# The last level of a block inverse in 32 by 32 blocks, inside the scan of a recurrent model

## The reference, cut to what matters

```
D_MODEL = 1024; SEQ = 512; DEPTH = 2; CHUNK = 64; HEAD_SIZE = 64; N_HEADS = 8

def wkv7_scan(r, w, k, v, kk, a):
    # state (B, H, N_v, N_k):
    # S_t = S_{t-1} (diag(w_t) - kk_t^T (a_t*kk_t)) + v_t k_t^T ;  y_t = S_t r_t
    def step(state, inp):
        r_t, w_t, k_t, v_t, kk_t, a_t = inp
        sk = einsum('bhvk,bhk->bhv', state, kk_t)
        state = (state * w_t[:, :, None, :] - sk[..., None] * (a_t * kk_t)[:, :, None, :]
                 + v_t[..., None] * k_t[:, :, None, :])
        return state, einsum('bhvk,bhk->bhv', state, r_t)
    ...
```

## Time and profile before

| | us |
|---|---|
| median of three runs | 3784.06 |
| lowest, highest | 3781.48, 3784.39 |
| the profiled execution, its own time | 3784.52 |
| its span, first to last instruction | 3782.7 |

### The profile page before, as it was taken

The page is one execution under the profiler, slowest core; times in us unless marked ns, Lnnn a source line. Parts: engine busy times, 40 slices in busy tenths (PEclk is TensorE's granted clock), DMA queues, the critical chain, the costliest instruction groups (busy, mean ns, idle before and its releaser), DMA issues. The chain is left out here.

```text
span 3782.7 us, 57931 instructions
## 1 busy us (share of the span) xinstructions
PE 3664.8 (97%) x24033; PEld 3028.9 (80%) x24033; DVE 2174.3 (57%) x2934; ACT 1367.3 (36%) x1537; POOL 0.2 (0%) x4
## 2 busy tenths in 40 slices
PE   7999999999999999999999998999999998899998
PEld 6788888888877888888887768888887768888887
DVE  6898466774369964667634565553234575553233
ACT  5554433432264544343323341133223351123223
POOL 0000000000000000000000000000000000000000
PEclk9999999999999999999999999999999999999999
DMA  3322223553322222245522420123232320032321
GB/s 112 87 73 62 78 89 110 202 189 122 94 78 81 67 68 78 94 151 189 198 89 71 132 79 26 36 101 99 90 100 81 111 99 26 25 111 89 100 94 73
DMA packets 272985, 364.68 MB, mean 96 GB/s; under 512 B 22428, under 2 KB 218640, under 8 KB 271504
## 3 DMA queue, kind: packets, MB, share of 16 engines
q1 hardware_dynamic: 247824, 311.45, 25.7%
q10 hardware_dynamic: 24960, 50.33, 3.8%
HBM read 351.79 MB, written 9.96 MB: 96 GB/s over the span
## 5 line engine op out<-in xcount | busy, mean ns | idle before, releaser
L248 PE MATMUL banks<-act_hi,w_hi 128*128 128x512 f32 x4208 | 1675.2, 398 | 32.1 <-issue 9.9
L250 PE MATMUL banks<-act_hi,w_lo 128*128 128x512 f32 x4208 | 1647.9, 392 | 0.0
L249 PE MATMUL banks<-act_lo,w_hi 128*128 128x512 f32 x4208 | 1647.5, 392 | 0.0
L170 DVE TENSOR_TENSOR w_lo<-w_raw,w_hi 128x2048 fp32r<-128x2048 f32 (+1 forms) x280 | 629.4, 2248 | 666.8 <-ACT w_hi L164 662.6
L248 PEld LDWEIGHTS banks<-act_hi,w_hi 128*128 128x128 f32 x4208 | 795.5, 189 | 237.1 <-issue 59.0
L250 PEld LDWEIGHTS banks<-act_hi,w_lo 128*128 128x128 f32 x4208 | 794.7, 189 | 169.9
L249 PEld LDWEIGHTS banks<-act_lo,w_hi 128*128 128x128 f32 x4208 | 796.0, 189 | 165.1 <-issue 4.3
L164 ACT ACTIVATE w_hi<-w_raw 128x2048 fp32r<-128x2048 f32 (+1 forms) x280 | 526.5, 1881 | 932.8 <-PE banks L250 891.4
L2064 DVE SCALAR_TENSOR_TENSOR arena<-arena,small 128x512 f32<-128x512 f32 (+1 forms) x168 | 126.3, 752 | 15.6 <-issue 4.3
L248 PE MATMUL banks<-w_hi,act_hi 128*128 128x256 f32 x384 | 110.3, 287 | 3.2 <-DVE w_lo L170 3.2
L249 PE MATMUL banks<-w_lo,act_hi 128*128 128x256 f32 x384 | 108.6, 283 | 0.0
(11 more groups left out here) (363 smaller groups left out, 3592.7 us busy)
## 6 DMA issues: line engine op xcount, KB each, us to landing
w_raw<-in_w_in SPq DMA_DIRECT2D x98, 1024.0 KB, 5.4
w_raw<-in_ffn_up SPq DMA_DIRECT2D x48, 1024.0 KB, 5.4
arena<-in_ada_w ACTq DMA_DIRECT2D x24, 2048.0 KB, 8.0
w_raw<-in_w_gu SPq DMA_DIRECT2D x44, 1024.0 KB, 5.0
w_raw<-in_ffn_down SPq DMA_DIRECT2D x24, 1024.0 KB, 4.8
w_raw<-in_w_down SPq DMA_DIRECT2D x20, 1024.0 KB, 5.0
w_raw<-in_w_out SPq DMA_DIRECT2D x16, 1024.0 KB, 4.9
w_raw<-in_w_branch SPq DMA_DIRECT2D x12, 1024.0 KB, 5.0
```

What stands on the lines that cost most here:

```text
L170: self.core.nc.vector.tensor_tensor(view(self.lo[:, s]), view(self.raw[:, s]), view(self.hi[:, s]).bitcast(FP32), ALU.subtract)\
L248: nc.tensor.matmul(out, wh, ah, start=first, stop=False)
L249: nc.tensor.matmul(out, wh, al, start=False, stop=False)
L250: return nc.tensor.matmul(out, wl, ah, start=False, stop=last)
```

## The change

At the last level (size 32) only one quarter of a head's matrix changes, and only the transpose of X is read later. The new code treats that level by itself, behind a loop over the first four:

- W is computed as one 32 x 32 product per head instead of one of 64 x 64. `quarters(h)` gives the upper and the lower 32 partitions of a head; the product reads the upper and writes the lower.
- VectorE copies that quarter into W for each of the two `h` (two instructions on 32 partitions with 4 blocks of 32 columns each) instead of one masked instruction on 128 x 256, and signals through a drain instead of with the instruction.
- The product into the first half of X is gone. The one into the transpose is 32 x 32 per head.
- VectorE subtracts it from the upper right quarter of the transpose, again in two instructions of 32 partitions.

The count and the order of the semaphores stay as they were.

```diff
+        def quarters(h):
+            return slice(64 * h, 64 * h + 32), slice(64 * h + 32, 64 * h + 64)
+
@@ pe_part
-                for n, lv in enumerate(LEVELS):
+                for n, lv in enumerate(LEVELS[:4]):
...
+                for cc in (0, 1):
+                    pe.wait_ge(x_ok, 12 * g + 8 + cc + 1)
+                    for pr, h in pairs:
+                        top, low = quarters(h)
+                        col, o = (cc * NP + pr) * CH, pr * CH
+                        last = nc.tensor.matmul(ps[low, w_bank[cc], o:o + 32], AT[top, col + 32:col + 64],
+                                                XX[cc][top, o:o + 32], start=True, stop=True)
+                    last.then_inc(w_ps, 1)
+                for cc in (0, 1):
+                    pe.wait_ge(w_ok, 10 * g + 8 + cc + 1)
+                    for pr, h in pairs:
+                        top, low = quarters(h)
+                        col, o = (cc * NP + pr) * CH, 256 + pr * CH + 32
+                        last = nc.tensor.matmul(ps[top, x_bank[cc], o:o + 32], W[low, col:col + 32],
+                                                XX[cc][low, o:o + 32], start=True, stop=True)
+                    last.then_inc(x_ps, 1)
@@ dve_part
-                for n, lv in enumerate(LEVELS):
+                for n, lv in enumerate(LEVELS[:4]):
...
+                left = lambda v: as3(v)[:, :, 0:32]
+                right = lambda v: as3(v)[:, :, 32:64]
+                for cc in (0, 1):
+                    dve.wait_ge(w_ps, 10 * g + 8 + cc + 1)
+                    for h in (0, 1):
+                        low = quarters(h)[1]
+                        nc.vector.tensor_copy(left(half(W, cc)[low]), left(ps[low, w_bank[cc], 0:256]))
+                    dve.drain().then_inc(w_ok, 1)
+                for cc in (0, 1):
+                    dve.wait_ge(x_ps, 10 * g + 8 + cc + 1)
+                    for h in (0, 1):
+                        top = quarters(h)[0]
+                        xt = right(XX[cc][top, 256:512])
+                        tt_(xt, xt, right(ps[top, x_bank[cc], 256:512]), ALU.subtract)
+                    dve.drain().then_inc(x_ok, 1)
```

## The result

| | before | after |
|---|---|---|
| median, us | 3784.28 (20 runs, 3779.97 to 3788.84) | 3790.41 (20 runs, 3786.82 to 3793.81) |
| profiled execution, us | 3784.52 | 3789.69 |

The ratio is 1.0017 with a 95% interval of 1.0011 to 1.0023. The change makes the kernel 6.1 us slower, where 5.2 us faster was forecast. The forecast was wrong in its sign, and the time lies outside its range (3775.5 to 3786).

The account below looks back on a forecast made before the run. TensorE and VectorE alternate in the last level, so savings there should reach the end in full: 3.53 - 2.88 = 0.65 us, 8 times, 5.2 us; 3784.5 - 5.2 = 3779.3 us (50%), own range 3776.5 to 3782, 8 in 10 3775.5 to 3786.

Parts of the forecast that it names:

- The sum: Timeline of the new last level: 2.88 us in place of 3.53, 0.65 us saved 8 times, 5.2 us.
- VectorE's pair: Two last-level instructions on different 32-partition groups, taken at 0.58 us with no overlap and no pause; ends 0.50 and 0.70.
- The row's overlap of 0.08 us: Profile row of two VectorE instructions on the same partitions, starting 0.34 us apart though one takes 0.42.
- (b): Rival, 16%: VectorE's pairs in the last level overlap as on equal partitions, 6.6 to 7.8 us faster.
- (c): Rival, 14%: VectorE's second instruction waits as behind a drain, or small tiles cost more; 1.4 us faster to 2.3 slower.
- The burst: TensorE's 16 records per chunk in the last level, taken at 0.73 us; range 0.52 to 0.73, or 1.16.
- TensorE's clock: Step on the granted clock halving behind thin TensorE stretches in the scans; a fall costs 1.05 us.
- one argument: Against a clock fall: if 32-column records start no closer, the last level's array streams as long, 2.0 us of 3.8.
- The other argument: Against a clock fall: the last level has no 2 us pause like the one at L2820 to L2822.
- (a): Rival, 20%: clock falls behind the thin last level, 1.05 us or more each; in all eight groups 3.2 to 6 slower.
- the case of bursts of 1.16 us: If two heads' small tiles no longer ran side by side in the last level: 0.29 us more, 2.3 us slower in all.
- The 0.2% line: Total time: differences within 0.2%, 7.6 us, can't be told from no change; "the same" was given 82%.

Follow-up runs that it names:

- e10_large_pause: e2_large with 24 extra unread 64x64 matmuls in TensorE's pause of L2820 to L2822: median 3771.17 us, ratio 0.9962 to the kernel before.
- e4_stream64: The change with its 32x32 weights, but each last-level matmul streams 64 columns in place of 32: median 3785.19 us, ratio 1.0003 to the kernel before.
- e6_cols32: The change with 64x64 weights in the last level's products, still streaming 32 columns: median 3783.81 us, ratio 1.0001 to the kernel before.
- the four corners: The change (32x32 weights, 32 columns), e4_stream64, e6_cols32 and e2_large: medians 3790.41, 3785.19, 3783.81 and 3776.48 us.
- e7: The kernel before with 24 extra unread 64x64 matmuls in TensorE's pause of L2820 to L2822: median 3777.73 us, ratio 0.9983.
- e3_drop: The kernel before with only the last level's unused product left out, and the update on the transpose's 256 columns alone: median 3776.03 us, ratio 0.9978.
- e8: e3_drop with 24 extra unread 64x64 matmuls in TensorE's pause of L2820 to L2822: median 3768.06 us, ratio 0.9959 to the kernel before.
- e2_large: The change with TensorE's last-level products back to 64x64 and 64 columns, unused product still out, VectorE's quarters kept: median 3776.48 us, ratio 0.9976.
- e1_fill: The change with eight extra unread 64x64 matmuls behind each last-level burst, sixteen behind the last: median 3782.34 us, ratio 0.9994 to the kernel before.
- e9_after_pause: The change with 24 extra unread 64x64 matmuls in TensorE's pause of L2820 to L2822: median 3781.96 us, ratio 0.9993 to the kernel before.

## Why the prediction was wrong

**The sum was right.** VectorE's pair was taken at 0.58 us. Two pairs of copies with a drain's gap of 0.12 between take 1.31 us, so a pair is 0.595; two pairs of updates take 1.27, so 0.575. One instruction is 0.29 or 0.28. The groups by line and shape of the kernel after:

```profile
L2858 DVE COPY arena<-banks 32x128 f32<-32x128 f32 x32 | 9.3, 290 | 2.1
L2865 DVE TENSOR_TENSOR arena<-arena,banks 32x128 f32<-32x128 f32 x32 | 9.0, 280 | 2.1
```

The row's overlap of 0.08 us is gone when the partitions change. That is what the rule of the Trainium skill says (VectorE: DVE Perf Modes, section Two Vector instructions with no wait between them); the trace agrees, with 0.595 us for two copies of 0.290. The level came to 2.89 against 2.88, and (b) and (c) fell with it.

**The burst was taken too long, at no cost.** 0.73 us was used, with the last start 0.46 us in; measured, that start is 0.25 us in (0.44 less 0.19). VectorE sets the level's length, so it didn't matter.

**What failed is the step "TensorE's clock".** It found the mechanism, in the earlier trace rows, and gave it 20%. The sum of the forecast has no term for the clock: 3779.3 counts 8 x 0.65 us saved and nothing for falls behind the level. The runs showed a fall in eight of eight groups, and 18.2 us more in the two scans than with the same level and no fall (288.7 against 270.5 in e10_large_pause), against 5.1 saved. The prediction let one argument hold the chance down: that if small records start no closer than large ones, the array streams as long as before and the clock holds. Two things were wrong in that. The change's records do start closer (15 starts in 0.25 us, against 0.46). And where they don't, in e4_stream64 and e6_cols32 (0.64 and 0.66 a burst), the clock fell all the same. The rule cited there is that a matmul of one column takes as long as one of 60 (the Trainium skill, TensorEngine Tiling (Array Packing), section Instruction Overhead). That 32 columns keep the pace of 64 was the prediction's step from it. The traces bear that out for 64x64 weights (0.66 us a burst in e6_cols32 against 0.68) and not for 32x32: 0.44 in the change against 0.64 in e4_stream64, or on average 17 ns from start to start in the change's burst against 31 for 64x64 with 64 columns. The other argument, that the level holds no pause of 2 us as the L2820 stretch does, carried nothing: a stretch of short bursts did more than the pause (falls in eight of eight groups, against five). What exactly about the small products lets the clock fall stays open beyond the four corners.

**The price of (a) came out near the measured time in part by luck.** 1.05 to 1.4 us a fall was set; one behind the level costs 1.45 (35.32 - 33.87). The forecast for falls in all eight groups was 3.2 to 6 us slower, and 6.1 was measured. Two terms that it had not worked against each other: the falls behind the last group of a layer last 10 us, some three times as long as most others, and cost 3.1 us each; and three of the falls behind the pause went, which gave something back. An estimate from these rows: 6 x 1.45 + 2 x 3.1 less 3 x 1.05 and less the 5.1 saved is about 6.6 us slower.

**In sum**, in the two scans: the kernel before takes 280.73 us, and 275.59 without its falls behind the pause (e7), -5.1. The level of 2.9 us without a fall (e10) makes it 270.50, another -5.1, where 5.2 was forecast for the level. The falls of the change take it to 288.67, +18.2. That is +7.9 for the scans; the rest of the span, which has the same code, was 2.8 us shorter in the change's profiled execution, and the medians are 6.1 apart.

**A slip in the sum**, with no weight: in the case of bursts of 1.16 us, X at 3.12 gives an update to 3.70 and L2756 at 3.78, not 3.74 and 3.82.

**The 0.2% line.** The measured +0.17% lies inside it, so "the same" was the case that came, but by way of (a) and not of the forecast; and the interval excludes no change.

## What to carry to other kernels

Making TensorE's products smaller in a stretch where another engine sets the pace saved nothing there, and in this kernel it cost the clock of the stretch behind it. In such a place try first to leave them large, and to take away only what shortens the chain. When a trace shows the granted clock falling behind one thin stretch, ask of each edit whether it makes another, and weigh that first and not last. In such a kernel idle TensorE time can be worth filling: 24 matmuls a group that nobody reads took 5 us off the scans of the kernel before. And where the rest of a long program varies by more than the change is worth, measure the stretch that was changed beside the total.

## What the runs showed that was not expected

- Work that is read by nothing made three kernels faster. By the medians it is 6.9 us on the kernel before (e7), 8.0 on e3_drop (e8 against e3) and 5.3 on e2_large (e10 against e2, on different chips); in the scans of the profiled executions it is 5.1, 3.0 and 1.2 us.
- With 64x64 weights and 64 columns the clock held behind the last level in eight of eight groups; with 32 in one of the two dimensions it fell in six, at bursts of nearly the same length (0.64 to 0.68 us).
- Changing between 32x32 and 64x64 tiles has a price where TensorE has no wait: in e1_fill 0.12 to 0.15 us lie between the last start of one and the first of the other, where records of one size follow each other by 0.02 to 0.03 on average. It showed in no total: in e9_after_pause the groups without a fall take as long as in e10_large_pause.
- In the change the clock stayed at half for 10 us behind the last group of each layer (2416 to 2426), where TensorE has no products of a next group and waits for VectorE in between; behind the other groups it was back within 7 us.
